# Routing in two parts and a first norm without scaled rows, in a hybrid attention and mixture-of-experts layer

## The reference

```python
h = rms_norm(x, g_mix) * (1 + sc1) + sh1                # the first norm
x = x + gt1 * token_mixer(h, ...)                       # q, k, v, gates: h @ w_in; three dilated
                                                        # attentions, one windowed; merged @ w_out
h = rms_norm(x, g_ffn) * (1 + sc2) + sh2
x = x + gt2 * hier_moe(h, ...)
out = rms_norm(x, g_final)

def hier_moe(t, ...):                                   # cut
    glog = t @ w_group + b_group                        # 4 groups
    gsel = argmax(glog); gw = softmax(glog)[gsel]
    elog = (t @ w_route + b_route)[group gsel]          # 8 experts of the group
    topw, topi = top_k(softmax(elog), 2)
    expert = gsel * 8 + topi                            # 2 of 32 experts for each token
    # the 4096 (token, expert) pairs are sorted by expert into blocks of 128 rows,
    # each expert's rows padded to whole blocks; every block:
    y = (silu(xb @ w_gate[e]) * (xb @ w_up[e])) @ w_down[e]
    # and each token adds its two rows, weighted with topw * gw
```

## Time and profile before

| | |
|---|---|
| median of 3 runs | 2830.72 (2829.3 to 2832.85) |
| the profiled execution | 2828.76 |
| its span, first to last instruction | 2825.8 |
| PE busy | 2643.8 (94%) |
| DVE busy | 1683.3 (60%) |
| ACT busy | 1514.0 (54%) |
| POOL busy | 913.4 (32%) |

### The profile page before, as it was taken

One profiled execution on the slowest core, in us unless ns is written; L12 is line 12 of the kernel. 1 busy time (PEld: TensorE's weight loads), 2 busy tenths in 40 slices (PEclk: granted clock), 3 DMA queues, 4 the chain that ended last, 5 costly groups with the idle time before them and its releaser, 6 DMA issues.

```text
span 2825.8 us, 44996 instructions
## 1 busy us (share of the span) xinstructions
PE 2643.8 (94%) x14050; PEld 2192.5 (78%) x14051; DVE 1683.3 (60%) x2956; ACT 1514.0 (54%) x2813; POOL 913.4 (32%) x756
## 2 busy tenths in 40 slices
PE   4999999999999978999999999289999999999968
PEld 3889989999777757888888888178888888888753
DVE  6777565545777765464522555668775535385856
ACT  6555777776665644443432222157665535375756
POOL 4555555566222233444434211011111111111115
PEclk8999999999999989999999999599999999999988
DMA  6222222111000033344343544279886746486997
GB/s 261 62 64 65 68 62 68 29 30 30 23 20 13 14 100 116 121 144 137 128 137 122 186 153 144 99 261 362 325 321 239 279 148 238 148 337 244 381 387 328
DMA packets 191115, 451.94 MB, mean 160 GB/s; under 512 B 36110, under 2 KB 86326, under 8 KB 188940
## 3 DMA queue, kind: packets, MB, share of 16 engines
q1 hardware_dynamic: 171980, 389.46, 39.1%
q0 software_dynamic: 14400, 52.44, 5.0%
q10 hardware_dynamic: 4608, 8.39, 0.8%
HBM read 380.01 MB, written 70.21 MB: 159 GB/s over the span
## 4 chain that ended last, share of the span: by engine, by line
PE 76%; DVE 8%; issue 5%; DMA 5%; ACT 4%; SPq 1%; POOL 1%; ACTq 0%; DVEq 0%; POOLq 0%
PE bank L1958 16%; PE bank L2263 15%; PE bank L2145 6%; PE bank L2190 4%; PE S_ps L2274 4%; PE E_ps L2274 4%; DMA sb_w_in<-in_w_gate_up 3%; PE S_ps L2145 3%; PE E_ps L2145 3%; PE O_ps L2000 2%; PE S_ps L1988 2%; PE S_ps L2084 2%; PE O_ps L2156 1%; PE S_ps L2156 1%; PE S_ps L2190 1%
## 5 line engine op out<-in xcount | busy, mean ns | idle before, releaser
L848 POOL TENSOR_TENSOR sb_h_lo<-sb_hT,sb_h_hi 128x512 fp32r<-128x512 f32 x256 | 372.3, 1475 | 487.5 <-ACT sb_h_hi L979 487.5
L2263 PE MATMUL bank<-sb_gu,sb_x_hiT 128*128 (+1 forms) x1568 | 494.2, 397 | 11.6 <-DVE sb_x_loT L1830 8.6
L1958 PE MATMUL bank<-sb_w_hi,sb_h_hi 128*128 128x384 f32 x1024 | 363.5, 355 | 1.5 <-DVE sb_hT L1415 0.9
L2263 PEld LDWEIGHTS bank<-sb_gu,sb_x_hiT 128*128 128x128 f32 x1568 | 293.2, 189 | 74.2 <-issue 11.2
L1958 PE MATMUL bank<-sb_w_hi,sb_h_lo 128*128 128x384 f32 x1024 | 343.6, 336 | 0.0
L1958 PE MATMUL bank<-sb_w_lo,sb_h_hi 128*128 128x384 f32 x1024 | 343.4, 335 | 0.0
L1816 DVE TENSOR_TENSOR sb_gu<-sb_w_in,sb_gu 128x1024 f32 (+1 forms) x256 | 300.8, 1220 | 64.8 <-ACT sb_gu L1268 62.9
L1268 ACT ACTIVATE sb_gu<-sb_w_in 128x1024 f32 (+1 forms) x256 | 257.1, 1059 | 109.2 <-DMA sb_w_in<-in_w_gate_up 83.2
L897 POOL TENSOR_TENSOR sb_g_lo<-sb_g_raw,sb_g_hi 128x1408 fp32r<-128x1408 f32 x64 | 211.5, 3325 | 310.5 <-ACT sb_g_hi L1075 310.5
L2263 PE MATMUL bank<-sb_gu,sb_x_loT 128*128 (+1 forms) x784 | 307.3, 392 | 0.0
L1114 ACT ACTIVATE sb_e_sb<-sb_e_sb,sb_o_row 128x256 f32<-128x256 f32 (+2 forms) x320 | 167.2, 525 | 152.7 <-DVE sb_o_row L1540 106.2
(11 more groups left out here) (406 smaller groups left out, 5984.7 us busy)
## 6 DMA issues: line engine op xcount, KB each, us to landing
sb_w_in<-in_w_gate_up SPq DMA_DIRECT2D x256, 512.0 KB, 6.3
sb_w_in<-in_w_expert_down SPq DMA_DIRECT2D x128, 512.0 KB, 5.4
sb_g_raw<-in_w_gb SPq DMA_DIRECT2D x64, 704.0 KB, 4.1
sb_late_w<-in_w_ada SPq DMA_DIRECT2D x64, 256.0 KB, 2.8
sb_yp<-y_d SPq DMA_DIRECT2D x16, 1024.0 KB, 21.6
sb_w_raw<-in_w_qkv SPq DMA_DIRECT2D x112, 96.0 KB, 2.0
sb_x_round<-in_x SPq DMA_DIRECT2D x4, 2048.0 KB, 17.8
sb_hT<-in_w_ada SPq DMA_DIRECT2D x4, 2048.0 KB, 18.0
```

What stands on the lines that cost most here:

```text
L848: nc.gpsimd.tensor_tensor(h_lo[c][:, ks], tile_src(g, T, ks), h_hi[c][:, ks].bitcast(F32), ALU.subtract).then_inc(sem("h_lo_ready"), 1)
L1958: last = nc.tensor.matmul(bank[c][:, 0:PASS_COLS].rearrange("p (a m) -> p a m", a=1), x[c][:, k, :], w[:, ds(row + k, 1), :], start=(k == ...
L2263: last = nc.tensor.matmul(PS[j][:].rearrange("p (a n) -> p a n", a=1), x[:, k, :], gu[:, ds(gu_row(e, part, k), 1), j * DE:(j + 1) * DE], ...
```

## The change

First norm: `scale_rows` is gone. DVE makes, for each tile, `scaler` = identity times the tile's inverse roots, and PE multiplies the unscaled block with `scaler` where it transposed the scaled block with the identity. ACT's and DVE's orders change. Routing: DVE chooses the experts of tiles 0 to 11 before it takes tile 12's logits and makes the residual of tile 14, and those of tiles 12 to 15 after the last logits; the steps are the same, on slices. The bias is loaded with the rows at the start of w_out, `rows_in` is awaited at 80, and `iota_e` is made before `zero_rows`. The weights `pair_w` are made behind the one-hots, `expert_of` behind the row tables, with a second count of `tables_ready`. In the experts `rows_low(0)` moves ahead of the sixth of the eight subtractions. Some tiles move in SBUF (the chosen tables now lie where `o_hi` and `o_lo` were).

```diff
@@ -78,6 +76,7 @@
 CHUNKS = SEQ // CHUNK
 TILES = CHUNK // P
 NJOBS = 6
+FIRST_CHOSEN = 12
 FIRST_MERGES = 3
...
@@ -220,6 +219,7 @@
     sq1 = m0("sq1", [P, D])
     mod_sum = [m0(f"mod_sum{c}", [P, CHUNK]) for c in range(FIRST_MOD - 1)]
     mod_row = m0("mod_row", [1, CHUNK])
+    scaler = Plan(w_hi_at + KD * PASS_COLS * 4)("scaler", [P, TT, P])
...
@@ -722,6 +728,7 @@
         for n, (t, row) in enumerate(((gt1b, 2), (A2b, 4), (B2b, 3))):
             sp.dma_start(t[:], rows_d[row:row + 1, :].broadcast_to([P, D])).then_inc(sem("rows_in"), 16)
         sp.dma_start(w_rt[:], A["w_rt"].rearrange("(k p) n -> p k n", p=P)).then_inc(sem("rows_in"), 16)
+        sp.dma_start(r_bias[:], A["b_rt"][0:1, :].broadcast_to([P, GROUPS + E])).then_inc(sem("rows_in"), 16)
         x_tile_in(1, 1)
         sp.wait_ge(sem("zero_rows"), 1)
         sp.dma_start(h2_d[SEQ:SEQ + PAD_ROWS // 2, :], zero_rows[:]).then_inc(sem("pads_out"), 16)
@@ -750,7 +757,6 @@
         sp.wait_ge(sem("logits_ready"), TT)
-        sp.dma_start(r_bias[:], A["b_rt"][0:1, :].broadcast_to([P, GROUPS + E])).then_inc(sem("rows_in"), 16)
         wgu_v = A["w_gate_up"].rearrange("e (k p) n -> p e k n", p=P)
...
@@ -904,8 +910,10 @@
             pool.wait_ge(sem("m_hi_ready"), t + 1)
             nc.gpsimd.tensor_tensor(m_lo[c][:], m_in[c][:], m_hi[c][:].bitcast(F32), ALU.subtract).then_inc(sem("m_lo_ready"), 1)
+        exact = dict(allow_small_or_imprecise_dtypes=True)
         lower_tile_out(0, 0)
         pool.wait_ge(sem("gates_done"), CHUNKS * KD + 2)
+        nc.gpsimd.iota(iota_e[:], pattern=[[0, TT], [1, E]], base=0, channel_multiplier=0, **exact).then_inc(sem("iota_ready"), 1)
         nc.gpsimd.memset(zero_rows[:], 0.0).then_inc(sem("zero_rows"), 1)
         lower_tile_out(1, 1)
...
@@ -996,13 +1002,6 @@
             at = slice(ROUND * q, ROUND * (q + 1))
             nc.scalar.activation(rms1[:, at], ssq1[:, at], ACT.Sqrt, bias=eps_col, scale=1.0 / D).then_inc(sem("rms"), 1)
-        def scale_rows(q):
-            act.wait_ge(sem("rstd"), q + 1)
-            for r in range(ROUND):
-                if r not in DVE_ROWS[q]:
-                    row = x_round[q][:, r, :]
-                    nc.scalar.activation(row, row, ACT.Copy, scale=rstd1[:, ROUND * q + r:ROUND * q + r + 1]).then_inc(sem("xn_act"), 1)
         def take_blocks(q):
             act.wait_ge(sem("columns"), 1)
@@ -1017,7 +1016,6 @@
         act.wait_ge(sem("ident_ready"), 1)
         squares(0)
-        scale_rows(0)
         act.wait_ge(sem("reduced"), 1)
         nc.scalar.activation(turn[:], ang[:], ACT.Abs).then_inc(sem("reduced"), 1)
...
@@ -1026,17 +1024,14 @@
         act.wait_ge(sem("mod_rows"), 1)
         nc.scalar.activation(mod_row[:], PS[7][0:1, :], ACT.Copy).then_inc(sem("mod_row"), 1)
         squares(1)
-        scale_rows(1)
         take_blocks(0)
         for i in range(KD // 2):
             raise_first(i)
         squares(2)
-        scale_rows(2)
         take_blocks(1)
+        squares(3)
         act.wait_ge(sem("h_all"), KD // 2)
         raise_tile(0, 0, 0)
-        squares(3)
-        scale_rows(3)
         take_blocks(2)
         take_blocks(3)
...
@@ -1320,6 +1315,7 @@
         next_expert_high(0, 0, range(KD))
         block_tail(0)
         down_high(0, 0)
+        act.wait_ge(sem("tables_ready"), 2)
         with act.Fori(1, total) as g:
             e = act.value_load(expert_of[0:1, ds(g, 1)], min_val=0, max_val=E - 1)
...
@@ -1407,6 +1396,10 @@
             dve.wait_ge(sem("rms"), q + 1)
             at = slice(ROUND * q, ROUND * (q + 1))
             nc.vector.reciprocal(rstd1[:, at], rms1[:, at]).then_inc(sem("rstd"), 1)
+            dve.wait_ge(sem("ident_ready"), 1)
+            dve.wait_ge(sem("rstd"), q + 1)
+            for t in range(ROUND * q, ROUND * (q + 1)):
+                nc.vector.tensor_scalar(scaler[:, t, :], ident[:], rstd1[:, t:t + 1], None, ALU.mult).then_inc(sem("scalers"), 1)
         def take_blocks(q):
@@ -1437,15 +1430,12 @@
         for j in range(FIRST_MOD):
             if j != PE_CHUNK:
                 add_chunk(j)
-        row_stats(1)
         take_columns()
         take_blocks(0)
-        scale_rows(1)
+        row_stats(1)
+        take_blocks(1)
         row_stats(2)
-        scale_rows(2)
-        take_blocks(1)
         row_stats(3)
-        scale_rows(3)
         for q in range(2, ROUNDS):
             take_blocks(q)
         dve.wait_ge(sem("attn_consts"), 1)
...
@@ -1709,56 +1699,65 @@
             dve.wait_ge(sem("logits_done"), t + 1)
             nc.vector.tensor_copy(logits[:, ds(t, 1), :], PS[6][:, 0:GROUPS + E].rearrange("p (a n) -> p a n", a=1)).then_inc(sem("logits_ready"), 1)
+        def choose(at):
+            nt = at.stop - at.start
+            def wide(ap, n):
+                return ap[:, at, :].broadcast_to([P, nt, n])
+            def flat(ap):
+                return ap[:, at, :].rearrange("p t a -> p (t a)")
+            def first_best(vals, n, best, eq, idx, oh_out):
+                link(nc.vector.tensor_reduce(flat(best), vals, AX.X, ALU.max))
+                link(nc.vector.tensor_tensor(eq[:, at, :], vals, wide(best, n), ALU.is_equal))
+                link(nc.vector.scalar_tensor_tensor(eq[:, at, :], eq[:, at, :], -float(n), iota_e[:, at, 0:n], ALU.mult, ALU.add))
+                link(nc.vector.tensor_reduce(flat(idx), eq[:, at, :], AX.X, ALU.min))
+                link(nc.vector.tensor_tensor(oh_out[:, at, :], eq[:, at, :], wide(idx, n), ALU.is_equal))
+            dve.wait_ge(sem("logits_ready"), at.stop)
+            rb = r_bias[:].rearrange("p (a n) -> p a n", a=1).broadcast_to([P, nt, GROUPS + E])
+            link(nc.vector.tensor_tensor(logits[:, at, :], logits[:, at, :], rb, ALU.add))
+            gl = logits[:, at, 0:GROUPS]
+            first_best(gl, GROUPS, gmax, geq, gidx, gsel)
+            link(nc.vector.tensor_tensor(gex[:, at, :], gl, wide(gmax, GROUPS), ALU.subtract))
+            if at.stop == TT:
+                dve.sem_inc(sem("differences"), 1)
+            link(nc.vector.tensor_scalar(gsel[:, at, :], gsel[:, at, :], -NEG, NEG, ALU.mult, ALU.add))
+            pen = gsel[:, at, :].rearrange("p t (g a) -> p (t g) a", a=1).broadcast_to([P, nt * GROUPS, PER_GROUP])
+            link(nc.vector.tensor_copy(el[:, at, :], logits[:, at, GROUPS:]))
+            el3 = el[:, at, :].rearrange("p t (g a) -> p (t g) a", a=PER_GROUP)
+            link(nc.vector.tensor_tensor(el3, el3, pen, ALU.add))
+            first_best(el[:, at, :], E, top[0], eeq, eidx, oh[0])
+            link(nc.vector.scalar_tensor_tensor(el[:, at, :], oh[0][:, at, :], 2 * NEG, el[:, at, :], ALU.mult, ALU.add))
+            first_best(el[:, at, :], E, top[1], eeq, eidx, oh[1])
+            link(nc.vector.tensor_tensor(both[:, at, :], oh[0][:, at, :], oh[1][:, at, :], ALU.add))
+            if at.stop == TT:
+                dve.sem_inc(sem("both_ready"), 1)
+            link(nc.vector.tensor_tensor(ratio[:, at, :], top[1][:, at, :], top[0][:, at, :], ALU.subtract))
+            if at.stop == TT:
+                dve.sem_inc(sem("differences"), 1)
         residual(0, 0, 0)
         residual(1, 1, 0)
-        with dve.Fori(1, TT // 2) as i:
+        with dve.Fori(1, TT // 2 - 1) as i:
             for c in range(2):
                 take_logits(2 * i + c - 2)
                 residual(2 * i + c, c, i)
+        dve.wait_ge(sem("iota_ready"), 1)
+        dve.wait_ge(sem("dve_chain"), ch.n)
+        choose(slice(0, FIRST_CHOSEN))
+        for c in range(2):
+            take_logits(TT - 4 + c)
+            residual(TT - 2 + c, c, TT // 2 - 1)
         take_logits(TT - 2)
         take_logits(TT - 1)
-        dve.wait_ge(sem("rows_in"), 80)
+        choose(slice(FIRST_CHOSEN, TT))
...
-        rb = r_bias[:].rearrange("p (a n) -> p a n", a=1).broadcast_to([P, TT, GROUPS + E])
-        link(nc.vector.tensor_tensor(logits[:], logits[:], rb, ALU.add))
-        gl = logits[:, :, 0:GROUPS]
-        def wide(ap, n):
-            return ap[:].broadcast_to([P, TT, n])
...
         link(nc.vector.tensor_tensor(pbase[:], pend[:], nblk[:], ALU.subtract))
         link(nc.vector.tensor_scalar(pbase[:], pbase[:], float(BLK), None, ALU.mult))
-        pe_b = pend[:].rearrange("p (a e) -> p a e", a=1).broadcast_to([P, MAX_BLOCKS, E])
-        ib_b = iota_b[:].rearrange("p (b a) -> p b a", a=1).broadcast_to([P, MAX_BLOCKS, E])
-        link(nc.vector.tensor_tensor(cmp_e[:], pe_b, ib_b, ALU.is_le))
-        link(nc.vector.tensor_reduce(e_f[:], cmp_e[:], AX.X, ALU.add))
-        link(nc.vector.tensor_scalar(e_f[:], e_f[:], float(E - 1), None, ALU.min))
-        link(nc.vector.tensor_copy(expert_of[0:1, 0:MAX_BLOCKS], e_f[0:1, :]))
...
@@ -1798,6 +1790,12 @@
             link(nc.vector.tensor_tensor(blk_at, wide_rows(iota_b, MAX_BLOCKS), blk_f[:, :, k:k + 1].broadcast_to([P, TT, MAX_BLOCKS]), ALU.is_equal))
             nc.vector.tensor_tensor(id_at, blk_at, flat_id[:, :, k:k + 1].broadcast_to([P, TT, MAX_BLOCKS]), ALU.mult)
```

(50 more changed lines are left out.)

56 lines of the change are left out of this document (4 added, 52 removed).

## The result

The changed kernel takes 2814.41 (median of five, 2814.2 to 2817.21) against 2829.3 for the kernel before, measured in turn with it: a ratio of 0.9946, interval 0.9935 to 0.9957, or 12 to 18 us less. Measured once more beside other kernels it took 2811.59 against 2830.55, a ratio of 0.9937 (0.9924 to 0.995). The two together make some 16.5 us. Forecast were 21.1 and 2809.6: the change is faster, inside the range, and short of the sum by 4 to 5 us. The profiled execution has a span of 2811.9, 13.9 less than that of before.

A forecast was written before the change was run, and what follows sets the result against it. PE bounds most slices; the change touches three stretches where PE waits: first norm, start of w_out, routing. 6.5 - 0.3 - 0.2 + 15.1 = 21.1 gained, so 2809.6 for the median; range 2805 to 2819.

The forecast's parts named there:

- First norm: Unscaled rows and products with scaler start the first projection at 77.2 instead of 83.67: 6.5 gained.
- DVE has its scalers by 65.4: First norm: after the last squares end at 64.4, four scalers and their reciprocal take 1.0 on DVE.
- PE pauses only some 1 us before these ten: First norm: short pause before PE's last ten product blocks, against 7 us before, so mostly full clock; 77.2 taken.
- Rival (a): First norm: the last ten product blocks run at the low clock, 2.0 lost instead of 6.5 gained, 2818; chance 0.17.
- (c): First norm: a product costs four transposed blocks, 1.76 at full clock; 10.5 lost, 2826; chance 0.04.
- (d): First norm: products of 3.5 a block, four transposed ones at the low clock throughout; 2865; chance 0.03.
- Bias: Start of w_out: DVE's first residual waits for five loads instead of four; 0.3 lost.
- Choice of twelve: w_out: choosing twelve tiles takes 10.5 on DVE, fitting with nothing to spare; 0.2 lost.
- Four tiles after the logits: Routing: choosing the last four tiles takes 6.3, so PE starts at 1786.8 instead of 1796.65: 9.9 gained.
- Table of experts: Routing: cmp_e to expert_of leave the chain ahead of the row tables: 5.1 gained.
- T + 15.3: PE's first expert block starts 15.3 after the row tables are ready (T, 1810.9), so 15.1 gained from the routing.
- rival (b): Routing: pieces 6 and 7 hold ACT, PE starts at T + 18.5 or all 5.1 go: 2813 to 2815; chance 0.11.

The follow-up runs named there:

- experiment 4: Changed kernel with one move: ScalarE raises tile 0 behind the takes of round 2, not ahead of them; a single run gave 2805.47.
- chosen_late: Changed kernel with all sixteen tiles chosen after the last logits, none during w_out; 2818.04, 0.9961 of the kernel before.
- tables_ahead: Changed kernel with the table of experts made ahead of the row tables again, as in the kernel before; 2817.56, 0.9957 of the kernel before.
- rows_early: Changed kernel with ScalarE raising the gathered rows before pieces 6 and 7 of the first expert; 2807.61, 0.992 of the kernel before.
- pieces_first: Changed kernel with gathered rows raised before pieces 6 and 7, and pieces 0 and 1 lowered ahead of the table of experts; 2808.05, 0.9935 of the kernel before.

## Why the prediction was right, and where it was not

**First norm, 6.5 forecast, 1.9 in the first profile, 2.7 on average: the term that was mis-sized.** The mechanism (unscaled rows, scalers, products of 0.9) was right. The step that failed is "DVE has its scalers by 65.4". It priced four tensor_scalars by DVE rows that had POOL idle beside them. It overlooked that the change moves `raise_tile(0, 0, 0)` behind `squares(3)`, so that POOL's subtraction starts at the very moment when DVE makes the last scalers. That cost 2.1 there. The price could have been read before: the 3.27 in place of 1.23 shown at experiment 4 stands in the trace of the kernel before. The next step fell with it: "PE pauses only some 1 us before these ten" became a pause of 3.05, and the clock fell for a pair. Of the 4.56 between 77.2 and 81.76, 2.1 are the scalers, and 1.76 are the last root, which came late (66.16 for 64.4). What is left is 0.7: the pair at the low clock cost 1.75, where the forecast had 0.5 in it for the clock, and the tail behind the ten blocks was priced some 0.6 too dear. The root was late because inputs landed a microsecond later in this execution (round 1's rows at 39.20, 38.16 before) and because six product blocks, two of them at the low clock, stand ahead of the modulation's columns on PE, which the prediction did not count. That is the scatter of this execution: over the seven the last root ends at 63.4 to 66.2, mean 64.5, as forecast, while the first projection's mean of 80.5 is still 3.3 late. Rival (a) had the mechanism, but not its extent: one of the five pairs at the low clock, and in two of the seven executions much of a second (2.98 and 3.19), but never all. With tile 0 raised later, in five executions, the first projection is at 75.5 to 77.2. The forecast's 77.2 is about what this first norm gives without the collision (two of the five have DVE's takes moved as well).

**The product's price.** Confirmed by 1.79 and 3.54 a pair; rivals (c) and (d) fall. Twice a transposed block it is.

**Bias.** 0.3 forecast as lost, 0.27 seen. What the sum counted only inside the 9.9 was the other side: 3.1 of them are the bias no longer waited for, as `chosen_late` shows.

**Choice of twelve.** 10.5 forecast, 10.6 seen, hidden but for about 0.1.

**Four tiles after the logits: 9.9 forecast, 9.7 seen. Table of experts: 5.1 forecast, 5.2 to 5.3 seen** in the end of the row tables (`tables_ahead`).

**Block 0: T + 15.3 forecast, T + 16.2 and T + 15.9 seen.** The mechanism was the one named, ACT held by piece 7 behind the 5.1 that were moved; rival (b) lies in the same place with a higher price. The landing was sized at 3.6 and was 5.0 and 4.7. The prediction saw this wait and took it as given; `rows_early` shows that it was worth 3.5 to 3.8 at block 0, and 4 at the end within some 5, for the order of two calls. So one of the prediction's own signs of being wrong, ACT waiting for a weight piece while gathered rows stand ready, was there to see; it had priced most of that wait, and missed 0.6 to 0.9 of it.

**Through to the end.** From block 0 to the end of the span it is 984.5 before and after, as argued. In sum: 2.7 - 0.3 - 0.1 + 14.5 = 16.8, beside some 16.5 measured. The time lies in the stated range because the range was drawn to take in rivals (a) and (b), and both bit in part. Two bounds of the prediction do not come out of its terms: 7.5 gained in the first norm (the full clock throughout gives 76.7, which is 7.0), and 2825 for all worst bounds (with the bias's whole 3.82 and block 0 at T + 18.5 they give some 2827). What stays open is the scatter of single executions between the first projection and w_out (the head start against the kernel before changed by -3.2 to +1.3 us there); it was not tried to remove it.

## What to carry to other kernels

Before pricing a small VectorE step by its own rows, look at what GpSimd does in that very stretch after the change: a call moved on a third engine can bring the two together. When a wait is removed ahead of a queue, ask which call at the head of the next engine's queue waits for something that the waiting work does not need, and let that call go second: here two such moves on ScalarE were worth some 7 us beside the change's 16.5. A gain of 2 us in a kernel of 2800 is not to be read from one execution, and ratios of five runs bounded a gain here only to some 3 us to either side; what told the causes apart were the marks of one stage, read from several executions.

## What the runs showed of the hardware

VectorE beside GpSimd: four 128x128 tensor_scalars took 0.87 alone and 2.91 beside two subtractions of 2.55 together, and ended with them; a 128x1024 addition took 1.23 alone and 3.27 beside one of 2.59. The Trainium skill ("SBUF — State Buffer", SBUF: two separate sides) has VectorE and GpSimd share one pair of ports as an exclusive lock: a VectorE step in a two-port mode, or one with two SBUF inputs beside a GpSimd step that reads SBUF, waits out the other's whole instruction if that started first. The addition, with its two SBUF inputs, agrees: it started 0.40 behind GpSimd's and ended 1.08 after it. The added 2.0 of the scalers agrees as well, if they run in such a mode, which no run here shows.

The first block's gather beside weight loads: 4.2 in the changed kernel, 7.2 to 7.5 where 512 KB pieces were issued at the same time (`pieces_first`, `tables_ahead`).

TensorE's clock: behind the pauses of 2.74 to 4.37 ahead of round 2's last pair, that pair took 3.35 to 3.79 in all seven executions with the change's own order, the low level's price, in place of 1.95. Behind 1.09 it took 2.05, the full level's, and behind 2.33 it took 2.05 in one execution and 2.92 in another.
